# A two-block transformer kernel on one core: input statistics ahead of the modulation chunks, and a mixing stage by seven block products that shares one program with the tail

## The reference, cut to what matters

```python
# first block, layer 0 (c, c_ctx: two vectors of 1024)
shift, scale, gate = jnp.split(jax.nn.silu(c) @ w_mod + b_mod, 3, axis=-1)
h  = rms_norm(x, norm_w)   * (1.0 + scale[:, None, :]) + shift[:, None, :]
hc = rms_norm(ctx, norm_w) * (1.0 + scale_c) + shift_c
p  = h @ w_in
...
# second block (o_b: output of the sparse attention, y_a: output of the linear attention)
y_b = o_b @ w_dsa_proj[i]
gate_a, gate_b = jnp.split(x @ w_in[i], ...)       # two of its parts, 1024 columns each
mixed = (jax.nn.sigmoid(gate_a) * y_a + jax.nn.sigmoid(gate_b) * y_b) @ w_out[i]
x = layer_norm_2(DEEPNORM_ALPHA * x + mixed, ln1_g[i], ln1_b[i])
# then the feed-forward part (w_up, causal convolution, w_down), a gated input p, two more layer norms
```

## Time and profile before

| | |
|---|---|
| median of 3 runs | 5003.1 us (5001.62 to 5003.62) |
| the profiled execution | 4999.76 us, its span 4998.0 us |
| PE busy | 4650.9 us (93%), 19278 records |
| DVE busy | 2182.8 us (44%) |
| ACT busy | 1312.8 us (26%) |
| mean granted clock of PE | 0.971 |

### The profile page before, as it was taken

The page is one execution under the profiler, slowest core; times in us unless marked ns, Lnnn a source line. Parts: engine busy times, 40 slices in busy tenths (PEclk is TensorE's granted clock), DMA queues, the critical chain, the costliest instruction groups (busy, mean ns, idle before and its releaser), DMA issues. The chain is left out here.

```text
span 4998.0 us, 47375 instructions
## 1 busy us (share of the span) xinstructions
PE 4650.9 (93%) x19278; PEld 2508.4 (50%) x19278; DVE 2182.8 (44%) x3676; ACT 1312.8 (26%) x2000; POOL 38.1 (1%) x74
## 2 busy tenths in 40 slices
PE   7998799899898799898999999999999999999996
PEld 2554466664443467753445764555544444444442
DVE  4344555540115555521596230333310355555554
ACT  2002544430201544411301340333310121110023
POOL 1000000000000000000000000000000000000000
PEclk9999899999999899999999999999999999999998
DMA  5300000012010000010011001000001211111111
GB/s 215 112 30 21 1 1 1 1 38 92 21 38 30 1 1 1 1 61 31 21 38 38 30 17 39 17 18 13 18 30 46 72 55 42 42 42 42 67 47 63
DMA packets 46111, 186.87 MB, mean 37 GB/s; under 512 B 5024, under 2 KB 5024, under 8 KB 44128
## 3 DMA queue, kind: packets, MB, share of 16 engines
q1 hardware_dynamic: 35136, 131.09, 7.7%
q0 software_dynamic: 10784, 53.09, 2.9%
HBM read 174.72 MB, written 9.44 MB: 37 GB/s over the span
## 5 line engine op out<-in xcount | busy, mean ns | idle before, releaser
L412 PE MATMUL psum<-arena 128*128 128x512 f32 x3040 | 1203.5, 558 | 39.1 <-ACTq L396 23.0
L412 PEld LDWEIGHTS psum<-arena 128*128 128x128 f32 x3040 | 575.4, 189 | 665.2 <-issue 651.3
L1918 PE MATMUL psum<-arena 128*128 128x512 f32 x1736 | 746.5, 591 | 1.2 <-DVE arena L2208 1.2
L1918 PEld LDWEIGHTS psum<-arena 128*128 128x128 f32 x1736 | 327.6, 189 | 419.8 <-issue 416.4
L951 PE MATMUL psum<-arena 64*128 64x512 f32 (+3 forms) x1200 | 407.5, 538 | 18.0 <-ACT arena L906 14.1
L1037 DVE TENSOR_REDUCE arena<-psum 128x1 f32<-128x1280 f32 (+1 forms) x216 | 294.3, 1366 | 65.5 <-PE psum L951 65.5
L960 PE MATMUL psum<-arena 128*128 128x128 f32 x1968 | 292.9, 278 | 21.1 <-ACT arena L1013 19.8
L960 PEld LDWEIGHTS psum<-arena 128*128 128x128 f32 x1968 | 226.2, 141 | 170.1 <-issue 113.2
L1008 ACT ACTIVATE arena<-psum,arena 128x1280 f32<-128x1280 f32 (+1 forms) x216 | 266.2, 1233 | 140.6 <-DVE arena L1037 136.5
L1891 PE MATMUL psum<-arena 128*128 128x512 f32 x640 | 285.2, 606 | 17.5 <-ACT arena L2025 14.4
L2208 DVE TENSOR_TENSOR arena<-arena,psum 128x512 f32<-128x512 f32 x224 | 154.1, 688 | 301.2 <-PE psum L1918 295.5
(11 more groups left out here) (262 smaller groups left out, 4278.8 us busy)
## 6 DMA issues: line engine op xcount, KB each, us to landing
arena<-stream SPq DMA_DIRECT2D x240, 512.0 KB, 3.5
arena<-mod_t POOLq DMA_DIRECT2D x32, 512.0 KB, 4.6
arena<-mod_w POOLq DMA_DIRECT2D x4, 2048.0 KB, 25.6
arena<-x SPq DMA_DIRECT2D x4, 1280.0 KB, 16.3
arena<-x POOLq DMA_DIRECT2D x8, 640.0 KB, 5.4
x_mid<-arena POOLq DMA_DIRECT2D x8, 640.0 KB, 3.4
arena<-x_mid POOLq DMA_DIRECT2D x8, 512.0 KB, 4.3
out<-arena POOLq DMA_DIRECT2D x2, 2048.0 KB, 7.5
```

The lines of the kernel that those rows point to most:

```text
L412: last = nc.tensor.matmul(ps(slot * SLOT + c0, n), lhsT=sb(w + k * P, P), rhs=rhs(k, c0, n), start=k == 0, stop=k == nk - 1)
L1918: last = nc.tensor.matmul(ps(pair_bank(j, p), HALF), lhsT=lhsT(k), rhs=rhs(k), start=k == 0, stop=k == nk - 1)
```

## The change

1. Opening. `pe_open` makes statistics 0 to 5 before chunk 0, 6 and 7 between chunks 0 and 1, and then chunks 1, 2 and 3. ACT makes all eight squares, copies chunk 0, makes the root, and then copies chunks 1, 2 and 3.
2. Mixing stage. The loop and its barrier go. Its work becomes 8 pairs at the head of `PAIRS`: four pairs of gate tiles from x, then four pairs of tiles of the sparse projection from GR (tiles 6 and 7 first), by `pair_products` and `pair`, in the tail's program. ACT applies one sigmoid to both tiles of a gate pair; DVE multiplies and adds both tiles of a sparse pair (`mixed`) ahead of the next pair. The first pair's sums of data and weights are made at the stage's start.
3. The first `out2` block takes its k-tiles in the order 6, 7, 0, ..., 5 and waits for each.
4. The stage's weights are loaded by the tail's four buffers. The sums of the data are waited for one by one.

```diff
@@ pe_open @@
         for c in range(MODCHUNKS):
+            for k in (range(6), range(6, KD), (), ())[c]:
+                stat(k)
             t.eng.wait_ge(mod_in[c].sem, t.next(mod_in[c]))
...
-            for k in range(2 * c, 2 * c + 2):
-                s = t.tiles % 2
-                t.tiles += 1
-                t.eng.wait_ge(squares[s].sem, t.next(squares[s]))
-                for c0, n in chunks(TC):
-                    last = nc.tensor.matmul(ps(SLOT + c0, n), lhsT=con("ones", P), rhs=sb(TMP_AT + s * TC + c0, n),
-                                            start=k == 0, stop=k == KD - 1)
-                last.then_inc(squares_used[s].sem, 1)
@@ act_open @@
-        for c in range(MODCHUNKS):
-            square(2 * c)
-            square(2 * c + 1)
-            if c < MODCHUNKS - 1:
-                move(c)
+        for k in range(KD):
+            square(k)
+        move(0)
         act_root(t, TC)
-        move(MODCHUNKS - 1)
+        for c in range(1, MODCHUNKS):
+            move(c)
@@ mixing stage @@
-    def pe_mix(t):
-        g = BLOCKS["mix"]
-        with t.loop(KD, "mix"):
-            pe_block(t, g, 0, x_rhs, chunks(T))
-            pe_block(t, g + 1, 1, lambda k, c0, n: sb(GR_AT + k * T + c0, n), chunks(T))
...
+    MIX_PAIRS = 8
+    PAIRS = [("gate", m, 0) for m in range(4)] + [("sparse", m, 0) for m in (3, 0, 1, 2)] + [("up", PLAIN_FF + j, 0) for j in range(UP_PAIRS)] + [("down", m, g) for g in range(3) for m in range(KD // 2)]
+    DOWN_START = MIX_PAIRS + UP_PAIRS
+    GROUP_STARTS = {0: 0, 4: 1, MIX_PAIRS: 2, DOWN_START: 3, DOWN_START + KD // 2: 4, DOWN_START + KD: 5}
+    SUM_ORDER = {g: (1, 2, 3, 4) if g in (0, 2) else (3, 1, 2, 4) for g in range(6)}
...
     def consumed(n):
-        if n < PLAIN_BLOCKS:
-            return block_used, n + 1
+        mixed = 2 * MIX_PAIRS
+        if n < mixed:
+            return product_done, 7 * (n // 2 + 1)
+        if n < mixed + PLAIN_BLOCKS:
+            return block_used, n - mixed + 1
@@ pe_tail @@
+        def out2(q, v):
+            n = 2 * MIX_PAIRS + q
+            ev, value = tail_in(n)
+            t.eng.wait_ge(ev.sem, value)
+            for i, k in enumerate((6, 7, 0, 1, 2, 3, 4, 5)):
+                if q == 0:
+                    t.eng.wait_ge(mixed_done.sem, i + 1)
+                last = nc.tensor.matmul(ps(ring(q), HALF), lhsT=sb(tail_w(n) + k * P, P), rhs=sb(MIX_AT + k * T + v * HALF, HALF),
+                                        start=i == 0, stop=i == KD - 1)
+            last.then_inc(block_used.sem, 1)
...
-            t.eng.wait_ge(data_sums.sem, 4 * g + 4)
+            order = SUM_ORDER[g]
+            t.eng.wait_ge(data_sums.sem, 4 * g + 1 + order.index(2))
             t.eng.wait_ge(weight_sums.sem, 4 * j + 3)
             product(j, P6, ws(2), xs(2), nk)
+            t.eng.wait_ge(data_sums.sem, 4 * g + 1 + order.index(3))
             product(j, P7, ws(3), xs(3), nk)
+            t.eng.wait_ge(data_sums.sem, 4 * g + 4)
             product(j, P4, w(1, 1), xs(4), nk)
...
+        for j in range(MIX_PAIRS):
+            pair_products(j)
+        t.eng.wait_ge(product_read.sem, 6 * MIX_PAIRS)
@@ act_tail @@
+        def sigmoid(j):
+            t.eng.wait_ge(product_read.sem, 6 * (j + 1))
+            m = PAIRS[j][1]
+            nc.scalar.activation(sb(mix_gate(m), 2 * T), sb(PAIR_AT + j % 2 * 2048, 2 * T), ACT.Sigmoid).then_inc(gate_ready.sem, 1)
+        for j in range(MIX_PAIRS):
+            if 0 < j <= 4:
+                sigmoid(j - 1)
+            if 2 <= j < 5:
+                t.eng.wait_ge(gate_ready.sem, j - 1)
+            elif j >= 5:
+                t.eng.wait_ge(mixed_done.sem, max(2, 2 * (j - 5)))
+            first_copy(j)
@@ dve_tail @@
+        def mixed(j):
+            m = PAIRS[j][1]
+            if j == 4:
+                t.eng.wait_ge(gate_ready.sem, 4)
+            for s in range(2):
+                c, y = sb(PAIR_AT + j % 2 * 2048 + s * T, T), sb(MIX_AT + (2 * m + s) * T, T)
+                step(nc.vector.tensor_tensor(c, c, sb(mix_gate(m) + s * T, T), ALU.mult))
+                step(nc.vector.tensor_tensor(y, y, c, ALU.add), mixed_done)
+        data_sums_of(0, 1)
+        weight_sum(0, 3, True)
+        weight_sum(0, 1, True)
+        data_sums_of(0, 2)
+        weight_sum(0, 2, True)
+        data_sums_of(0, 3)
+        data_sums_of(0, 4)
+        weight_sum(0, 4, True)
+        for j in range(MIX_PAIRS):
+            if j > 4:
+                mixed(j - 1)
+            pair(j)
+        mixed(MIX_PAIRS - 1)
@@ SP @@
-        stream("stream", 2, BLOCKS["out2"] - 2)
+        stream("stream", 2, BLOCKS["mix"] - 2)
```

More of the change, by code:

```diff
@@ L471, in pe_open, with stat @@
     def pe_open(t):
+        def stat(k):
+            s = t.tiles % 2
+            t.tiles += 1
+            t.eng.wait_ge(squares[s].sem, t.next(squares[s]))
+            for c0, n in chunks(TC):
+                last = nc.tensor.matmul(ps(SLOT + c0, n), lhsT=con("ones", P), rhs=sb(TMP_AT + s * TC + c0, n),
+                                        start=k == 0, stop=k == KD - 1)
+            last.then_inc(squares_used[s].sem, 1)
         t.eng.wait_ge(act_to_pe.sem, t.next(act_to_pe))
         for c in range(MODCHUNKS):
+            for k in (range(6), range(6, KD), (), ())[c]:
+                stat(k)
             t.eng.wait_ge(mod_in[c].sem, t.next(mod_in[c]))
@@ L1801, in tail_loads @@
     def tail_loads():
+        mix = [BLOCKS["mix"] + m for m in range(2 * KD)]
         out2 = [BLOCKS["out2"] + m for m in range(KD)]
@@ L1806, in tail_loads @@
         ple = [BLOCKS["ple"] + m for m in range(KD)]
-        return out2 * 2 + first * 2 + rest + ple * 2
+        return mix + out2 * 2 + first * 2 + rest + ple * 2
     def consumed(n):
-        if n < PLAIN_BLOCKS:
-            return block_used, n + 1
+        mixed = 2 * MIX_PAIRS
[3 more added lines that the diff above has]
+            return block_used, n - mixed + 1
         if n < PLAIN_BLOCKS + 2 * len(PAIRS):
@@ L1823, in pair_load @@
     def pair_load(j, s=0):
-        return PLAIN_BLOCKS + 2 * j + s
+        return (PLAIN_BLOCKS if j >= MIX_PAIRS else 0) + 2 * j + s
     def weight_quarter(j, s, h):
@@ L1858, in group_of @@
     def group_of(j):
-        return 0 if j < UP_PAIRS else 1 + (j - UP_PAIRS) // (KD // 2)
+        return max(g for start, g in GROUP_STARTS.items() if start <= j)
     def pair_bank(j, p):
@@ L1865, in pair_out, with mix_gate @@
         return sb(PAIR_AT + j % 2 * 2048 + s * T + v * HALF, HALF)
+    def mix_gate(m):
+        return PAIR_AT + 2048 if m == 3 else A_AT + (16 + 2 * m) * T
     def ffn_count(tile):
@@ L1907, in product @@
         def product(j, p, lhsT, rhs, nk):
+            first = 7 * MIX_PAIRS if j >= MIX_PAIRS else 0
             r = 7 * j + p - 1
-            if r < 6:
-                t.eng.wait_ge(half_free.sem, PLAIN_BLOCKS - 5 + r)
-            elif r >= 8:
+            if first and r < first + 6:
+                t.eng.wait_ge(half_free.sem, PLAIN_BLOCKS - 5 + r - first)
+            elif r >= first + 8:
                 j0, p0 = (r - 8) // 7, (r - 8) % 7 + 1
@@ L1956, in pe_tail @@
                 bank_free(q)
-                plain(q, q, lambda k: sb(MIX_AT + k * T + v * HALF, HALF))
+                out2(q, v)
                 q += 1
@@ L1975, in pe_tail @@
                 q += 1
-        for j in range(len(PAIRS)):
+        for j in range(MIX_PAIRS, len(PAIRS)):
             pair_products(j)
@@ L2208, in combine, with weight_sum @@
             step(nc.vector.tensor_tensor(out, a, b, op), ev)
-        def weight_sum(j, i):
-            if j >= len(PAIRS):
+        def weight_sum(j, i, first=False):
+            if not first and j in (MIX_PAIRS, len(PAIRS)):
                 return
@@ L2254, in pair @@
         def pair(j):
-            up = PAIRS[j][0] == "up"
+            convolves = MIX_PAIRS < j <= DOWN_START
+            down = PAIRS[j][0] == "down"
             g = group_of(j)
-            turn = j + 1 in GROUP_STARTS
-            last = not up and PAIRS[j][2] == 2
+            turn = j + 1 in GROUP_STARTS and j + 1 != MIX_PAIRS
+            last = down and PAIRS[j][2] == 2
             p2, p6, p7, p4, p5, p3 = (ps(pair_bank(j, p), HALF) for p in (P2, P6, P7, P4, P5, P3))
@@ L2266, in pair @@
             combine(u2, s1, p6, ALU.add, product_read)
-            if 0 < j <= UP_PAIRS:
+            if convolves:
                 convolve(j - 1, 0)
-            if not up:
+            if down:
                 step(add_to(j, 0, 0, c11), residual)
@@ L2403, in _ @@
         for s in range(2):
[L2404 removed]
+            eng.wait_ge(w_loaded[s].sem, 8 * BLOCKS["mix"])
         for s in range(4):
@@ L2627, in pack_stream @@
         add(column_block(w, at2["gates"] + D + m * P))
+    for m in (6, 7, 0, 1, 2, 3, 4, 5):
         add(column_block(i["w_dsa_proj_2"][0], m * P))
```

83 lines of the change are left out of this document (33 added, 50 removed).

## The result

The changed kernel takes 4948.7 us (median of 4 runs, 4946.78 to 4949.73), the kernel before 5002.7 us in the same set; the ratio is 0.9892, with a 95% interval of 0.9877 to 0.9908. That is 54 us less. The forecast was 49.6 less, 4953.5; its range ended at 4949.0, 0.3 us above the median. The profiled execution took 4949.7 us (span 4948.0), 50.0 less than the profiled one of before.

The account below looks back on a forecast made before the run. PE, busy 93% of the span, was taken to bound the kernel. Mixing stage 31.4 plus opening 18.2 gave 49.6 us less: 4950.2 from the profiled execution, 4953.5 predicted from the median, range 4949 to 4961.

Parts of the forecast that it names:

- the stage's term: Mixing stage and its end: 200.7 us to DVE's first out2 step instead of 232.1, gain 31.4 us.
- made ahead in both: First up group after the stage: its data sums, in another order, are made ahead before and after; no gain counted.
- The base: Whole kernel: 49.6 us off the profiled 4999.8 gives 4950.2; the same step from the median 5003.1 gives 4953.5.
- The opening's term: Opening: PE starts at 10.2 instead of 16.81, first projection block at 65.2 instead of 83.48; gain 18.2 us.
- Two of the forecast's own signs of being wrong: Opening: clock at its lower level over statistics 4 and 5; projections ending less than 18 us earlier.
- rival B: Clock falls in the opening's 2.1 us hole or ahead of out2, or DVE late at first P6: 4955 to 4959; chance 0.22.
- no wait at the first P6: Mixing stage's first pair: PE waits 0.15 us for DVE's sums, bounds nothing and 2 us.
- DVE's work lies under PE's: Mixing stage: DVE's 13.0 us for a sparse pair fit under the 24.1 us that PE gives a pair.
- C: PE keeps full clock into the first projection block: 2.2 us more gain, 4951.3; chance 0.10.
- D: Opening: PE never reaches the upper clock level in its early start; opening gives 8.8 us, 4963; chance 0.05.
- E: Mixing stage: a pair's weights come late and the kernel is slower; each load must land 39 us after issue; chance 0.01.

Follow-up runs that it names:

- opening alone: The kernel before with the change's new opening only (`pe_open` and `act_open`): 4981.5 us, 20.4 less than before's 5002.0.
- the rest alone: The changed kernel with the opening of before, so new mixing stage and split waits only: 4966.3 us, 35.6 less than the kernel before.
- slow first chunk mended: The kernel before with six spare PE matmuls ahead of the first modulation chunk: 4999.9 us, 2.1 less, single times from 4998.2 to 5001.6.

## Why the forecast was off

The mechanism was right and the stage's term near its size; the time fell outside the range, by 0.3 us, which is less than a median is good to, because one edit had been priced at nothing without a look.

- **The failed step** is a term left out. "1736 records, 746.5 us busy with 1.2 us idle before them" was read for its pace, and the idle time passed over; and of the data sums past the stage the forecast said only that the first up group's are "made ahead in both". The row names DVE as releaser. It was one hole of 1.15 us (at 4534.15 in the trace of before, below), at the turn from up to down, where P6 waited for all four data sums though its operands need three, and the diff splits just this wait in every group. It is worth 3.5 or 3.6 us in three pairs of medians (5.5 in the fourth) and 3.3 in each of four pairs of traces: 1.4 at the turn, where the hole is 1.15, some 1.7 as a slow spell in the norm behind it, and the rest around that. With it, 4953.5 becomes 4950.0, inside the range.

```profile
4534.15 26.05 PE L1918 MATMUL psum<-arena 128*128 128x512 f32 x60 [1.15 <-DVE arena L2208]
```

- **The base.** The forecast put the 3.3 us between the profiled execution and the median on the changed kernel as well. From the traces, 2.1 of them lay in the old opening (a first chunk 0.67 us later and 1.45 longer in the second profile), which the change takes away. Without the 3.3 the same sum gives 4950.2. The 5003.1 itself, from three executions, lay 1.1 above the middle of the five sets. The opening's term is 20.5 and 20.4 between medians with the old stage, and 18.3 against that execution.
- **Luck.** Between the two profiled executions the forecast was 49.6 us less and 50.0 came out. That is not the sum come true. PE's lead was 16.3 us at the mixing stage (3643.32 - 3627.00) where 18.2 were forecast, 31.1 were added up to the first up block where 31.4 were forecast, and 2.6 came behind that, where nothing was: the part left out made good what the opening fell short of. Two of the forecast's own signs of being wrong were met in that profile, the lower clock over statistics 4 and 5, and projections less than 18 us ahead.
- **Opening.** Predicted 10.2, a hole from 21.0 to 23.1, 27.6, 60.0, 65.2; found 10.6, 21.1 to 23.0, 29.2 (27.6 in the second profile), 61.5 (59.9), 65.9 (64.3). The clock fell in the hole in two of the four profiles of the changed kernel's opening in the new program (1.93 and 1.85 us) and was kept in two (0.92 and 1.95), so rival B's condition was met in half of them. The transposes took 1.17 us and not 1.87; the granted clock over them is 1.00, and it was 0.50 before. The slow first statistics cost nothing in the end, since PE has to wait for the third x transfer behind them.
- **Stage.** 200.7 predicted to DVE's first out2 step, 201.0 found: 192.9 for the products, no wait at the first P6, 0.9 for the hole. From the stage's first matmul to the first up block the traces have 341.8 us before (3985.14 - 3643.32) and 310.7 after (3937.74 - 3627.00), 31.1 less; the medians give 29.6 to 32.1, the forecast was 31.4. That DVE's work lies under PE's is borne out, with 4.9 us a pair on top.
- **Rivals.** C didn't come by itself: the first block is 18.9 us and more unless PE is given work in the hole (17.4). D and E didn't come: PE reached full clock within the first four statistics, and the weights never made it wait.
- **Open.** In the medians, with the old opening, the split waits are worth 5.5 us in the new stage and 3.6 in the old one; so opening alone and the rest alone (20.5 + 35.7) add to 2.6 us more than the whole. The traces give the waits 3.3 in all four cases, so this excess has another place, and it is not found. By what way the wait brings on the slow spell is open too. Of the kernel before's scatter of 4 us, the two profiles put 2.1 in the first chunk; but with its slow first chunk mended, it still scatters by 3.4.

## What to carry to other kernels

Where a row that is to prove "nothing waits" holds a microsecond of idle time, find the instruction it stands before: a diff that splits or moves a wait may be aimed at it. Work out a forecast from the profiled execution, and ask which of the stages that differ between it and the median the change removes, before adding the difference back. When an engine has to wait for a transfer, look for work that is already there, as chunk 0 was, before reordering the rest around it.

## What the runs showed of the hardware that wasn't expected

The first chunk's slow start cost 1.4 us in one execution and 2.8 in the next (8.43 and 9.88 us against 7.04). The Trainium skill (TensorE: Matmul & The Clock Gate, Part 1: The HAM clock gate) says that such starts vary from run to run, and here the trace agrees. A hole of PE of the same length has either outcome: at the same place of the same opening, statistics 4 and 5 took 6.26 us behind a hole of 1.93 us and 4.58 behind one of 1.95, and the variance matmul behind 2.40 us ran at the lower level in two traces and at the upper one in seven. A wait of 1.15 us went with a slow spell 280 us later, in six traces against ten. Three spare matmuls of PE in the hole ahead of the first projection block kept the clock up in both runs that had them (17.44 us against 18.86 to 20.45); with a fourth elsewhere the kernel took 3.7 us less, not all of it in the opening.
